# One-hot rows of the first key in the gate matrix build, moved from VectorE to GpSimd

## What is computed

```python
v1, i1 = lax.top_k(s1, 16)            # per token and head, 128 first keys
v2, i2 = lax.top_k(s2, 16)            # 128 second keys
...
top_s, pos = lax.top_k(cand, 16)      # 16 of the 256 pairs
idx = take(i1 * 128 + i2, pos)
gates = softmax(top_s)
...
act = gelu(einsum("td,thkd->thk", hb, expert_down[idx]))
out = einsum("thk,thkd->td", gates * act, expert_up[idx])
```

## Time and profile before

| | us |
|---|---|
| median of 3 runs | 3124.64 |
| lowest, highest | 3124.26, 3128.69 |
| the profiled execution's own time | 3126.98 |
| its span | 3125.3 |

### The profile page before, as it was taken

One profiled execution on the slowest core, in us unless ns is written; L12 is line 12 of the kernel. 1 busy time (PEld: TensorE's weight loads), 2 busy tenths in 40 slices (PEclk: granted clock), 3 DMA queues, 4 the chain that ended last, 5 costly groups with the idle time before them and its releaser, 6 DMA issues.

```text
span 3125.3 us, 36151 instructions
## 1 busy us (share of the span) xinstructions
PE 2802.3 (90%) x12801; PEld 2193.1 (70%) x12801; DVE 1888.6 (60%) x3288; ACT 896.6 (29%) x1085; POOL 866.2 (28%) x547
## 2 busy tenths in 40 slices
PE   4993778899987789999999999599999899899997
PEld 1442434459985589999999887389777777678875
DVE  7605364759999977887888898540112754262342
ACT  1121111233336622333322222244212324332221
POOL 3000000115640034444343322033211124334442
PEclk8996579999999999999999999899878999999999
DMA  8420012443333389899889898122702442222221
GB/s 338 153 87 0 0 49 90 158 145 108 116 99 158 161 310 321 308 315 318 312 305 321 294 305 307 69 68 93 118 27 82 135 153 88 81 74 95 94 94 61
DMA packets 190239, 500.78 MB, mean 160 GB/s; under 512 B 30704, under 2 KB 79872, under 8 KB 188080
## 3 DMA queue, kind: packets, MB, share of 16 engines
q1 hardware_dynamic: 140528, 315.20, 30.6%
q0 software_dynamic: 49616, 184.42, 16.4%
HBM read 452.70 MB, written 46.86 MB: 160 GB/s over the span
## 4 chain that ended last, share of the span: by engine, by line
PE 57%; issue 19%; DVE 16%; POOL 4%; DMA 1%; DVEq 1%; ACT 1%; POOLq 0%; ACTq 0%; SPq 0%
PE psum L1352 17%; PE psum L1588 13%; PE psum L1343 11%; PE psum L495 6%; PE psum L514 5%; DVE arena L1633 5%; POOL l_r L794 4%; DVE arena L1636 2%; DVE arena L1640 1%; PE psum L1199 1%; DVE arena L1964 1%; DVE arena L1961 1%; DVE arena L1962 1%; PE psum L1256 1%; DVEq L1636 1%
## 5 line engine op out<-in xcount | busy, mean ns | idle before, releaser
L815 ACT ACTIVATE arena<-psum 128x512 f32 (+7 forms) x477 | 319.1, 681 | 1341.4 <-PE psum L1343 393.5
L1633 DVE TENSOR_TENSOR arena<-arena 128x384 f32<-128x384 f32 (+11 forms) x396 | 339.9, 861 | 523.5 <-ACT arena L815 300.5
L1352 PE MATMUL psum<-e_r,e_r 128*128 128x512 f32 x2304 | 542.7, 392 | 11.3 <-DVE e_r L1633 11.3
L794 POOL TENSOR_TENSOR l_r<-arena,l_r 128x1024 fp32r<-128x1024 f32 x144 | 350.8, 2437 | 725.9 <-ACT l_r L470 725.9
L1343 PE MATMUL psum<-e_r,e_r 128*128 128x384 f32 x2048 | 525.7, 337 | 11.5 <-POOL l_r L766 7.8
L1352 PEld LDWEIGHTS psum<-e_r,e_r 128*128 128x128 f32 x2304 | 433.9, 189 | 99.9 <-issue 9.0
L1343 PEld LDWEIGHTS psum<-e_r,e_r 128*128 128x128 f32 x2048 | 370.5, 188 | 25.8 <-POOL l_r L766 15.0
L815 ACT ACTIVATE e_r<-arena 128x1024 fp32r<-128x1024 f32 x256 | 270.2, 1057 | 361.5 <-PE psum L1352 344.7
L1343 PE MATMUL psum<-e_r,l_r 128*128 128x384 f32 x1024 | 344.0, 336 | 0.0
L778 POOL DMA_INDIRECT arena<-in_down_rows,arena x128 | 161.9, 1265 | 426.8 <-DMA scratch_gates<-arena 180.4
L778 POOL DMA_INDIRECT arena<-in_up,arena x128 | 163.6, 1278 | 278.3 <-DVE arena L2060 143.9
(11 more groups left out here) (199 smaller groups left out, 3483.5 us busy)
## 6 DMA issues: line engine op xcount, KB each, us to landing
arena<-in_down SPq DMA_DIRECT2D x128, 512.0 KB
arena<-in_up SPq DMA_DIRECT2D x128, 512.0 KB, 6.9
arena<-in_w_ada POOLq DMA_DIRECT2D x48, 512.0 KB, 8.2
scratch_gates<-arena SPq DMA_DIRECT2D x12, 2048.0 KB, 6.3
arena<-scratch_gates SPq DMA_DIRECT2D x32, 768.0 KB
arena<-in_w_in SPq DMA_DIRECT2D x44, 512.0 KB, 3.5
arena<-in_w_query SPq DMA_DIRECT2D x16, 512.0 KB, 3.5
arena<-in_w_glu SPq DMA_DIRECT2D x16, 512.0 KB, 3.5
```

Of the source, the lines that this page charges most:

```text
L794: nc.gpsimd.tensor_tensor(rr(lo, 1024, "l"), reg(RING + q % NSLOT * SLOT, 1024), rr(hi, 1024, "l").bitcast(F32), ALU.subtract).then_inc(S[ ...
L815: do(sc.activation(out, in_, f, **kw), sem)
L1352: last = mm(bank(2 * tt_ + hf), rr(w__ + tt_ * P, P), rr(x__ + hf * 512, 512), start=(first and n == 0), stop=(final and n == 2))
L1633: do(v.tensor_tensor(out, a, b, op), sem)
```

## The change

POOL now writes A. Behind its 48 subtractions and ahead of the gathers it waits for the slots, and then, for each of the 96 units, for `g_mm` as DVE does, makes four comparisons of 128x128 with one scalar column each, and counts a new semaphore `a_hot`. PE waits for `a_hot` too. DVE no longer writes A; it keeps the four comparisons that carry the gate. POOL's loop is written out, without registers.

```diff
@@ POOL @@
+            pool.wait_ge(S["slots_T"], S.base("slots_T") + 3)
+            for n in range(TD // 4):
+                pool.wait_ge(S["g_mm"], S.base("g_mm") + n + 1)
+                for t in range(4):
+                    last = nc.gpsimd.tensor_scalar(reg(OA + n % GB * 512 + t * P, P), con("iota"), reg(I1T + 4 * n + t, 1),
+                                                   None, ALU.is_equal)
+                last.then_inc(S["a_hot"], 1)
+
             rows_d, rows_u = io["down_rows"], io["up"].rearrange("j p n -> (j p) n")
             pool.wait_ge(S["idx"], S.base("idx") + 1)
@@ PE @@
                 for u_ in range(GB):
+                    pe.wait_ge(S["a_hot"], S.base("a_hot") + i * GB + (u_ + 1))
                     pe.wait_ge(S["b_hot"], S.base("b_hot") + i * GB + (u_ + 1))
@@ DVE @@
                     wait("g_mm", i * GB + (u_ + 1))
-                    tt(three(OA + u_ * 512, 4, P), bc(con("iota").unsqueeze(1), [P, 4, P]),
-                       bc(A[:, bass.ds(i * (4 * GB) + (I1T + 4 * u_), 4)].unsqueeze(2), [P, 4, P]), ALU.is_equal, FREE)
                     for t in range(4):
```

## The result

The changed kernel takes 3198.41 us (median of 4 runs, 3197.35 to 3203.85) against 3126.29 us before (4 runs in this comparison): a ratio of 1.0234, 95% interval 1.0216 to 1.0252. It is 72 us slower. The forecast was 3177 us with a range of 3105 to 3255, so the direction and the range held; the predicted loss of 50 us was 22 us short.

What follows compares the result with a forecast made beforehand. DVE bound the stage at 1.64 us a unit; Pool would bind it at 4 x (0.39 + 0.15) = 2.16 us, so 96 x 0.52 = +50 us on 3127 gives 3177 us, range 3105 to 3255.

Steps and rivals of the forecast that it cites:

- The bound and the cover: Gate-matrix stage, 929 to 1088 us: DVE binds, nothing else covers it, so the end moves one to one.
- its buffer loop: Pool's two buffers come back after 1.79 us a unit, under Pool's 2.16, so Pool never pauses.
- The price of a Pool comparison: Each 128x128 comparison on Pool: 0.39 us, from the full tensor_tensor rate plus a memset's fixed part.
- a turn: Each Pool comparison waits for a DVE instruction, as the engines alternate whole instructions: 0.15 us, at most 0.255.
- The fixed part: Share of a Pool comparison's price independent of columns: 0.10 us, as in Pool's smallest memsets.
- the upper end: Highest price for one Pool comparison, 0.59 us, with 0.30 us fixed from the gap between indirect DMAs.
- the cast of the earlier trace: DVE's 128x256 cast in the profile before: 1.48 to 1.79 us beside Pool, 0.295 with Pool idle.
- The clock: PE's clock in the stage might drop to 1.2 GHz, 1.89 us a unit; nothing charged.
- Rival 1: Pool comparison takes 0.15 to 0.25 us, turns included; bank loop binds, -37 us, 3090 us; chance 0.20.
- its floor: Loop of PE and ACT over two banks if Pool cost nothing: 1.25 us a unit, a gain of 37 us.
- Rival 2: No turns: Pool's 1.56 us a unit runs beside DVE, -8 us, 3119 us or no change; chance 0.10.
- Rival 3: Heavy fixed part: 0.59 + 0.15 us a comparison, 2.96 a unit, +127 us, 3254 us; chance 0.20.

Runs made afterwards that it cites:

- e5: Changed kernel with DVE's four comparisons per unit replaced by one memset of one column, so Pool has the stage to itself; 3196.3 us.
- e11: As e6, but DVE's comparisons replaced by one memset of one column, so Pool is alone; 3116.21 us.
- e2: Changed kernel with each Pool comparison writing 64 columns instead of 128; 3142.02 us.
- e8: Split of the change: Pool writes the rows of two tokens of each unit, DVE those of the other two; 3116.07 us, ratio to before 0.9955.
- e6: Changed kernel with one Pool comparison of 128x512 a unit in place of four of 128x128; 3120.2 us.
- e7: Kernel before without DVE's 128x512 comparison and with nothing in its place; 3106.95 us.
- e3: Changed kernel with Pool comparing against the constant 5.0 instead of a scalar column read per partition; 3203.27 us.

## Why the prediction was right, and where it was not

**The bound and the cover: right.** The stage was read as bound by DVE alone and as lying uncovered on the path to the end. It got 69.4 us longer, and the end moved by 71.1 us in span, of which 2.2 us is the store's other length.

**Pool becomes the bound, its buffer loop does not: right.** Pool is busy 224 of 226 us. Two buffers are enough although PE's unit takes 2.05 us, and by an estimate from the rows this was close: (2.37 + 0.13 + 2.05 + 0.13) / 2 = 2.34 us, 0.03 under Pool's 2.37.

**The price of a Pool comparison: the step that failed.** The sum had 0.39 us for the comparison and 0.15 us for a turn, together 0.54; it is 0.587 alone (e5) and 0.592 beside DVE. The two terms were wrong in opposite directions, and that they nearly cancelled is luck: with 0.39 us and no turn the same sum says 3119 us, faster than before, so the direction hung on a turn that isn't there. The fixed part was taken from a memset of one column, 0.10 us; it is 0.26 us (e5 and e11; 0.30 by e2, which DVE disturbs), and of the two candidates the gap of 0.30 us between indirect DMAs in the earlier trace rows was the better one, though nothing shows that the two have the same cause. The rate of 2.3 ns a column, taken over from the tensor_tensor of the earlier trace rows, was close to the 2.5 ns measured, although only one of the operands is a full tensor. In the upper end's 0.59 us the fixed part is a little high and the rate a little low: with it the sum without turns is 4 x 0.59 = 2.36 us, 96 x 0.72 = 69 us, which is what came. The estimate from the Trainium skill, 0.36 us a comparison (GPSIMD Engine Reference, sections 3.1 and 7), and by "roughly line-rate" (section 4.1) 0.11 us, both fall short of the measured 0.587; at 1.2 GHz the measured 2.5 ns a column are 3.0 cycles, where section 3.1 had 1.8 and the estimate by line rate 1.

**The turn: next to nothing for this pair.** The prediction carried it over from the cast of the earlier trace rows, on the ground that DVE's comparisons run at the same double rate. e5 shows 0.005 us for Pool, and DVE's median span was 0.346 us beside Pool, 0.389 before. After about a third of DVE's comparisons the next one did start 0.06 us late, which is the "apart by more than 0.255 us" of the prediction in a small size. What the sentence passed over is that in the earlier trace rows the Pool instruction had two full tensors and lasted 2.4 us, and that the other pairs of the earlier trace rows had a tensor_tensor on DVE's side too. e8 found the turn exactly there. How much two engines hold each other up changed with the width of Pool's comparison: at 64 columns both paid (e2), at 128 DVE a little and Pool hardly, at 512 DVE over half a microsecond a unit (e6). These sizes are measured; the mechanism is not.

**The clock: right for its effect.** The prediction had PE's clock falling and charged nothing. The granted clock fell from 0.98 to a mean of 0.67 of 2.4 GHz, units at the 1.2 GHz level took 2.05 us (granted clock 0.50 from 1003.5 to 1010 us), and Pool still did not pause. The prediction had taken 1.89 us for such a unit; with 2.05 its own loop gives (2.16 + 0.13 + 2.05 + 0.13) / 2 = 2.24, over its 2.16. That nothing was to be charged held because Pool was slower than predicted. Only the last unit paid, 2.06 us for 1.17. In e2 and e8, with units of 1.78 and 1.49 us, PE's passes have their short median of 0.275 us again.

**The rivals.** Rival 1 (Pool quick) would have needed 0.41 us a comparison; its floor was also reckoned too low, 1.25 us where e7 shows 1.40, because ACT's pauses between its evictions were not in the loop. Rival 2 had nearly the right mechanism, no turns, with the wrong price. Rival 3 had nearly the right price and added a turn that was not there: 3254 instead of 3198. The truth was rival 2's mechanism with rival 3's price.

## What to carry to other kernels

An idle engine is worth only what its instructions cost in the form needed: four instructions of 128x128 on Pool took 2.37 us where DVE made the same rows with one broadcast instruction in 0.61, so first see whether the move also splits one instruction into several, and pay the fixed part for each. Balance rather than move: with half of the rows on each engine Pool's slowness was hidden and the kernel gained 0.5%, less than the 0.7% forecast, in part because DVE was held up beside Pool. Before a gain is counted, work out the loop of the remaining engines with every wait in it, an engine's pauses between its own instructions included; here they left 20 us of the 37 to be had.

## What the hardware showed that was not expected

- A Pool tensor_scalar in float32, from start to start: 0.587 us for 128 columns (e5) and 1.556 for 512 (e11), both alone, so 2.5 ns a column and 0.26 us fixed; 0.446 us for 64 columns beside DVE (e2), of which 0.411 where nothing was in the way; 0.599 us for 128 columns with a constant in place of the scalar column (e3).
- Its profiled span can be shorter than its period: 0.528 us against 0.599 in e3, with Pool never waiting for another engine there.
- Pool's tensor_scalar of 128 columns beside DVE's tensor_scalar of 128x128: 0.592 against 0.587 us. Beside DVE's tensor_tensor of 128x256: 0.89 against 0.60 us (e8).
- DVE's tensor_scalar of 128x128 beside Pool's of 128 columns: after every third the next one starts 0.31 us later instead of 0.256 (e8, 96 of 288); all of these end 0.42 to 0.46 us after the start of a Pool comparison. Beside Pool's of 512 columns four take 1.58 us instead of 1.02 (e6).
- TensorE at a mean granted clock of 0.67 in a stage where it ran eight passes and then paused in each 2.37 us, and at 0.98 with the same passes in each 1.78 us (e2).
